# A gate table in memory: the last block's gates written by indirect transfers instead of one-hot products

## The reference, cut to what matters

```python
v1, i1 = lax.top_k(s1, 16); v2, i2 = lax.top_k(s2, 16)          # per token and head, over 128 keys each
cand = v1[:, None] + v2[None, :]; cidx = i1 * 128 + i2
top_s, pos = lax.top_k(cand, 16); eidx = cidx[pos]
gates = softmax(top_s)
act = gelu(u[eidx] . x)                                          # one number per token and chosen expert
y = sum over heads and choices of gates * act * v[eidx]
```

## Time and profile before

| | |
|---|---|
| median of 3 runs | 1862.31 us |
| the profiled execution | 1858.56 us |
| its span | 1856.8 us |
| PE busy | 1700.5 us (92%) |
| DVE busy | 1405.6 us (76%) |
| ACT busy | 694.7 us (37%) |
| POOL busy | 481.9 us (26%) |
| first and last rt_u_hi | 630.5 and 1277.1 us |

### The profile page before, as it was taken

The page is one execution under the profiler, slowest core; times in us unless marked ns, Lnnn a source line. Parts: engine busy times, 40 slices in busy tenths (PEclk is TensorE's granted clock), DMA queues, the critical chain, the costliest instruction groups (busy, mean ns, idle before and its releaser), DMA issues. The chain is left out here.

```text
span 1856.8 us, 28598 instructions
## 1 busy us (share of the span) xinstructions
PE 1700.5 (92%) x9877; PEld 1551.1 (84%) x9877; DVE 1405.6 (76%) x2543; ACT 694.7 (37%) x1050; POOL 481.9 (26%) x340
## 2 busy tenths in 40 slices
PE   6997778896879999999979998996999999999997
PEld 3875567554658899999979998996999999999996
DVE  4776766887342278999999998943888888888886
ACT  4664222325232234433334443432333333333333
POOL 1000000000110257877622332311332333322220
PEclk8999898888889999999989999998999999999999
DMA  3321000000213357887868887887999999999993
GB/s 107 101 81 55 1 1 35 23 1 1 91 57 101 129 156 241 291 274 264 269 222 322 324 322 257 321 291 270 330 369 393 371 377 380 374 369 335 355 348 107
DMA packets 149138, 404.56 MB, mean 218 GB/s; under 512 B 14100, under 2 KB 71700, under 8 KB 145592
## 3 DMA queue, kind: packets, MB, share of 16 engines
q1 hardware_dynamic: 108728, 243.99, 39.0%
q0 software_dynamic: 36864, 134.23, 19.1%
q10 hardware_dynamic: 3456, 25.17, 3.4%
HBM read 350.90 MB, written 52.44 MB: 217 GB/s over the span
## 5 line engine op out<-in xcount | busy, mean ns | idle before, releaser
L1579 PE MATMUL bank<-h_hi,rt_u_hi 128*128 128x384 f32 x1024 | 354.1, 346 | 24.7 <-DVE rt_u_lo L1364 13.4
L1744 PE MATMUL bank<-va_w_hi,va_v_hi 128*128 128x384 f32 x1024 | 342.9, 335 | 16.5 <-DVE va_w_lo L1695 16.5
L1581 PE MATMUL bank<-h_hi,rt_u_lo 128*128 128x384 f32 x1024 | 345.9, 338 | 0.1
L1580 PE MATMUL bank<-h_lo,rt_u_hi 128*128 128x384 f32 x1024 | 345.7, 338 | 0.0
L1745 PE MATMUL bank<-va_w_lo,va_v_hi 128*128 128x384 f32 x1024 | 342.7, 335 | 0.0
L1746 PE MATMUL bank<-va_w_hi,va_v_lo 128*128 128x384 f32 x1024 | 342.6, 335 | 0.0
L1294 ACT ACTIVATE rt_u_hi<-raw 128x1024 fp32r<-128x1024 f32 x128 | 135.7, 1061 | 385.9 <-PE bank L1581 385.6
L1672 ACT ACTIVATE va_v_hi<-raw 128x1024 fp32r<-128x1024 f32 x128 | 135.8, 1061 | 338.5 <-PE bank L1746 327.1
L1824 POOL DMA_INDIRECT h<-u_rows_dram,own_experts x128 | 172.0, 1344 | 279.5 <-DVE own_waste L1371 266.4
L1830 POOL DMA_INDIRECT qy<-v_dram,own_experts x128 | 129.8, 1014 | 373.1 <-DVE va_own L1722 368.4
L1579 PEld LDWEIGHTS bank<-h_hi,rt_u_hi 128*128 128x128 f32 x1024 | 195.2, 191 | 28.0 <-DVE rt_u_lo L1364 13.8
(11 more groups left out here) (328 smaller groups left out, 2733.5 us busy)
## 6 DMA issues: line engine op xcount, KB each, us to landing
raw<-u_dram SPq DMA_DIRECT2D x128, 512.0 KB, 4.1
raw<-v_dram SPq DMA_DIRECT2D x128, 512.0 KB, 7.0
active_scratch<-rt_act SPq DMA_DIRECT2D x128, 192.0 KB, 5.3
gates_scratch<-early ACTq DMA_DIRECT2D x24, 1024.0 KB, 7.4
early<-gates_scratch SPq DMA_DIRECT2D x16, 1536.0 KB, 12.4
early<-active_scratch SPq DMA_DIRECT2D x128, 192.0 KB, 7.6
in_raw<-w_in_dram SPq DMA_DIRECT2D x22, 512.0 KB, 3.4
query_raw<-w_query_dram SPq DMA_DIRECT2D x16, 512.0 KB, 3.5
```

The costliest lines, as they stand in the source:

```text
L1579: mm(bank, u_hi[:, j % 2, cols], hi[:, c, 0:TD], start=c == 0, stop=False)
L1580: mm(bank, u_hi[:, j % 2, cols], lo[:, c, 0:TD], start=False, stop=False)
L1581: last = mm(bank, u_lo[:, j % 2, cols], hi[:, c, 0:TD], start=False, stop=c == DC - 1)
L1744: mm(bank, v_hi[:, j, cols], w_hi[:, j, :], start=start, stop=False)
```

## The change

The table is built by one-hot products for two dense blocks only; the third dense block's gates go into the table by indirect transfers that add single elements in memory.

- Phase 1 has 32 steps (64 to 95, two bodies), phase 2 has 32 (96 to 127). All steps are written out; the hardware loop is gone from every engine but SP.
- Of the last block's slots no transpose, no `keep_slots` and no `split_gates` is made. `finish(3)` writes its gates to `single`, with tokens on partitions and slots along the row, and `list_experts(3)` computes for each slot its element number in the table, in two instructions (`place`).
- ACT issues, in step 19 (phase 0), one DMA that writes zeros over the last block's four chunks: 64 KB on each of 128 rows, 8.4 MB, from a zeroed buffer of 1 KB that is read 64 times.
- POOL issues 128 indirect DMAs, one per slot; each adds 128 elements of 4 bytes, one per token, to the table. They are put between the gathers: three behind each gather from gather 51 on. The first waits for the zeros, the places and the gates. Every 16th (one head's slots) waits until all before it have landed.
- SP waits for all 128 before it loads the gate table.
- The own dots: 48 in phase 0, 32 in phase 1 and 24 in phase 2 (12 per body).

```diff
+SPREAD = DENSE - 1
...
-    BODY, BODIES = 16, (4, DENSE, 1)
-    START = (0, 64, 112)
+    BODY, BODIES = 16, (NB, SPREAD, 2)
+    START = (0, 64, 96)
-    DOTS = (16, 16, 8)
-    FIRST_DOT = (0, 48, 96)
+    DOTS = (16, 16, 12)
+    FIRST_DOT = (0, 48, 80)
...
+        single, place = sb("single", [P, SLOTS]), sb("place", [P, SLOTS], U32)
+        empty = sb("empty", [P, 2 * P])
...
-            for j in range(BODY):
-                step(1, 0, j, True)
-            with eng.Fori(1, BODIES[1]) as i:
-                for j in range(BODY):
-                    step(1, i, j, False)
-            for j in range(BODY):
-                step(2, 0, j, True)
+            for phase in (1, 2):
+                for i in range(BODIES[phase]):
+                    for j in range(BODY):
+                        step(phase, i, j, i == 0)
...   (SP, after the last u loads)
-                    sp.wait_ge(sent[par], 16 * 2 * 2 * DENSE)
+                    sp.wait_ge(sent[par], 16 * 2 * 2 * SPREAD)
+                sp.wait_ge(s["scattered"], 16 * SLOTS)
...   (ACT)
-                    if phase == 1 and head and j == 4:
-                        keep_slots(NB - 1, t.bank[4])
+                    if phase == 0 and i == 1 and j == 3:
+                        act.wait_ge(s["empty"], 1)
+                        act.dma_start(gates_d[:, SPREAD * P // CH:TD // CH].rearrange("p c e n -> p (c e n)").rearrange(
+                            "p (k n) -> p k n", n=2 * P),
+                            empty[:].unsqueeze(1).to_broadcast([P, P * PK // (2 * P), 2 * P])).then_inc(s["cleared"], 16)
...   (POOL)
-                for k in range(START[1] - BODY, EARLY_DOTS + RING):
+
+                def scatter(k):
+                    if k == 0:
+                        pool.wait_ge(s["cleared"], 16)
+                        pool.wait_ge(s["places"], 1)
+                        pool.wait_ge(s["chosen"], NB)
+                    elif k % PTOP == 0:
+                        pool.wait_ge(s["scattered"], 16 * k)
+                    nc.gpsimd.indirect_dma_start(
+                        out=gates_d.rearrange("p c e (n one) -> (p c e n) one", one=1),
+                        out_offset=bass.IndirectOffsetOnAxis(ap=place[:, k:k + 1], axis=0),
+                        in_=single[:, k:k + 1], in_offset=None, compute_op=ALU.add).then_inc(s["scattered"], 16)
+
+                for at, k in enumerate(range(START[1] - BODY, EARLY_DOTS + RING)):
                     gather(k)
+                    for q in range(max(0, 3 * (at - 3)), min(SLOTS, 3 * (at - 2))):
+                        scatter(q)
...   (DVE)
+                    if i == NB - 1:
+                        place_f = num_f[:, 0].rearrange("p h k -> p (h k)")
+                        link(d.tensor_scalar(place_f, out[:, 0, :], float(TD * PK), t.vec[:, V_BASE:V_BASE + 1],
+                                             ALU.mult, ALU.add))
+                        d.scalar_tensor_tensor(place[:], out[:, 2, :], float(CH), place_f,
+                                               ALU.mult, ALU.add).then_inc(s["places"], 1)
...
-                    gates_out = out[:, 3, :] if i else gate_own[:]
+                    gates_out = (gate_own[:], out[:, 3, :], out[:, 3, :], single[:])[i]
...
+                d.memset(empty[:], 0.0).then_inc(s["empty"], 1)
...
-                    if phase == 1 and head and j == 6:
-                        split_gates(NB - 1)
...   (PE)
-                    if phase == 1 and head and j == 3:
-                        pe.wait_ge(s["moved"], 3)
-                        turn_slots(NB - 1, t.bank[4])
-                        pe.wait_ge(s["slots"], NB - 1)
```

More of the change, by code:

```diff
@@ L57 @@
 C_N = C_MT + LEVELS
-V_LN1, V_LN2, V_FIN, V_CONV, V_GDN, V_QN, V_KVN, V_IG, V_IB, V_EPS, V_ALOG, V_DTB, V_QK, V_ROWS, V_N = (
-    0, 8, 16, 24, 72, 73, 75, 77, 78, 79, 80, 84, 88, 96, 96 + 2 * 16)
+V_LN1, V_LN2, V_FIN, V_CONV, V_GDN, V_QN, V_KVN, V_IG, V_IB, V_EPS, V_ALOG, V_DTB, V_QK, V_ROWS, V_BASE, V_N = (
+    0, 8, 16, 24, 72, 73, 75, 77, 78, 79, 80, 84, 88, 96, 96 + 2 * 16, 97 + 2 * 16)
 CAND_ROWS = ((0, 1, 16), (1, 2, 8), (2, 4, 5), (4, 8, 3), (8, 16, 1))
@@ L1129, in route_stage @@
         "chain", "picked", "scores", "taken", "tops", "exps", "listed", "chosen", "turned", "slots_t", "slots",
-        "iota", "hots", "hot", "placed", "moved", "gelu", "kept")}
+        "iota", "hots", "hot", "placed", "moved", "gelu", "kept", "empty", "cleared", "places", "scattered")}
     with ExitStack() as ctx:
@@ L1155, in route_stage @@
         h_tok = t.pair
-        slot = sb("slot", [P, TD, 2, 2], BF16)
-        gate, rest = sb("gate", [P, TD]), sb("rest", [P, P])
-        piece = sb("piece", [P, 3, TD, 2], BF16)
+        slot = sb("slot", [P, SPREAD * P, 2, 2], BF16)
+        gate, rest = sb("gate", [P, SPREAD * P]), sb("rest", [P, P])
+        piece = sb("piece", [P, 3, SPREAD * P, 2], BF16)
+        single, place = sb("single", [P, SLOTS]), sb("place", [P, SLOTS], U32)
+        empty = sb("empty", [P, 2 * P])
         iota = sb("iota", [P, P], BF16)
@@ L1314, in step @@
                             send(i - 1, BODY + j - 2)
-                    if phase == 2:
+                    if phase == 2 and head:
                         if j < 2:
@@ L1929, in layout @@
     vec[:, V_ROWS:V_ROWS + 2 * PTOP] = row_tables()
+    last = SPREAD * P + np.arange(P)
+    vec[:, V_BASE] = last // CH * PK * CH + last % CH
     keys = np.stack([f["peer_sub_keys_1"][0], f["peer_sub_keys_2"][0]], axis=1)
```

## The result

The changed kernel takes 1931.13 us (median of 4 runs, 1926.39 to 1933.49), the kernel before 1861.87 us beside it: ratio 1.0365, 95% interval 1.0344 to 1.0386. 69 us slower where I had forecast 13 faster; the time lies 31 us above my range.

The account below looks back on a forecast made before the run. PE was taken to bound the kernel, with DVE close behind in phase 1. The terms -22.7 - 7.6 - 1.7 + 0.6 + 18 = -13.4 us gave 1845.2 profiled, 1849 us predicted as median; range 1829 to 1900.

Parts of the forecast that it names:

- Steps 1 to 5: Routing stage: sixteen steps' one-hot products -22.7 us, hardware loop -7.6, last block's transposes and slots -1.7, `place` +0.6, zero fill 0.
- Step 6, POOL's issue: Scatters on POOL between gathers: issues cost 0 in themselves, late start and waits for landings +18 us.
- POOL's issue: Rival, chance 0.12: 0.17 us more per issue makes groups miss low's end, 35 us more in phase 1, 1884 us.
- One gather and three scatters just fit a step: Phase 1 on POOL: four issues fit a 5.58 us step, with 0.67 us in hand that low takes back.
- The rule under it: On POOL, an indirect issue waits for DVE's tensor_tensor in progress, then takes 0.9 us beside the next.
- The waits every 16th: POOL's seven waits for landings, five in phase 1, taken at 4 us each: +18 us, with 2 us spare deducted.
- The start: Gather 52 goes 9.6 us late behind three scatters; of some 11.6 us to spare, 2 remain.
- Step 7: Scatters on the DMA engines, 1024 elements per engine: taken as 0, bounds 0 and +72 us.
- The fixed cost of a transfer: Estimate from the skill's page for the waits every 16th: 0.8 us each and 2 us lost.

Follow-up runs that it names:

- Plain writes: The changed kernel with scatters that write instead of add: 1888.03 us; with odd heads also sent to a second table (g 6.33 us): 1875.62 us.

## Why the prediction was wrong

**Steps 1 to 5 held.** Without scatters the change is worth 32.9 us, predicted 31.4; the loop 7.6 of it, as predicted; PE's wait at step 64 14.4 us, predicted 14.0. The zero fill landed after 74.5 us (predicted 71) with an issue of 0.44 us; I had taken 1.7 us for that issue. u loads beside it took 6.4 us in place of 3.9, and 7.6 at the longest, inside their time to spare. Neither the fill nor the sixteen steps were run alone, but nothing of the 32.9 us is missing, and in the run without scatters rt_u_hi starts every 4.16 us from step 98 on and every 5.58 in steps 68 to 71, as predicted.

**Step 6, POOL's issue, is the step that failed**, in three ways.

- *The price.* I gave a scatter the gather's 0.94 us because both have 128 indices. It takes 1.56. That the addition could cost was named in the rival, but only as the 0.17 us that would break the fit; it was 0.6. With it a group is over its time by its price alone: 0.94 + 3 x 1.56 and four gaps of 0.30 are 6.8 us, and 5.56 are there.
- *The fit.* "One gather and three scatters just fit a step" was a layout in which each issue arrived just before an instruction of DVE ended. Plain writes, with issues of 0.98 us, are the test: without waits for landings g is 6.33 us, and 6.41 between gathers 52 and 80, where POOL met no wait at all and the layout has 5.58. The rule under it was right. The scatter of 963.88 starts 0.1 us into a low, which ended at about 964.92, and is over at 966.44, 1.5 us later. That of 966.74 starts among the three gated instructions, 0.63 us each, close to the first one's end, and takes 1.55. The DVE rows for it:

```profile
963.78 1.22 DVE L1385 TENSOR_TENSOR rt_u_lo<-raw,rt_u_hi 128x1024 fp32r<-128x1024 f32 x1
964.92 1.22 DVE L1520 TENSOR_TENSOR qy<-rt_iota,rt_slot 128x2048 bf16<-128x2048 bf16 x1
966.17 1.90 DVE L1525 TENSOR_TENSOR qy<-qy,rt_piece 128x1024 bf16<-128x1024 bf16 x3
```

  But a wait of 0 to 1.1 us on each issue is a mean to be added, and not something that a layout makes vanish. In the changed kernel it is 0.12 us for a scatter and 0.38 for a gather, with plain writes 0.23 for a scatter.

  The Trainium skill ("SBUF — State Buffer", "Who interferes with whom") infers that a tensor_tensor doesn't stall descriptor generation; these rows are against it too.
- *The rival's price.* "POOL's issue" had the right mechanism and a chance of 0.12, but I priced it by a single missed boundary, 1.25 us a step, 1884. The rows I had would have bounded it: four issues of 1.81 us and four gaps of 0.30 make 8.4 us, against 5.56 an extra 2.9 us for each of 43 groups, and a high end beyond 1931. A range that ended at 1900 left that out. I also priced it for phase 1 alone, since phase 2 had 5.55 us for a group of 4.96; there a group took 7.4 (gathers 80 to 94).

**The waits every 16th** were sized well: 25.0 us in 6 places are 4.2 us each, I took 4 (the seventh met none), and taking them away gave 27 us. They didn't decide the outcome: POOL was over its time without them, and that run was still 2.1% slower than the kernel before. In *The start* 21.1 - 9.2 is 11.9 and not 11.6; it changes nothing.

**Step 7 held** for the scatters that add. The DMA share fell, from 0.88 to 0.79, gathers landed sooner than before, and clearings that send nothing lie on the same line as the scatters.

**The fixed cost of a transfer**, about 2 us in the Trainium skill ("DMA: Bandwidth & Descriptors", "Anatomy of one DMA — SWDGE (gpsimd) path"), would by my estimate have made the waits 0.8 us each; the six here were 0.7 to 6.3.

## What to carry to other kernels

Work moved to an engine that "has room" must be measured against the queue it joins: add up all that the queue must issue between two items that others wait for, at the dearest price that the trace shows for such an instruction, and compare it with the period of the consumer. Below the period it is free (1832 us), above it every tenth of a microsecond comes back times the number of groups (42 here), and the idle time that it makes can also cost the clock (31 of the 104 us). And where a change bundles several edits, run the cheap one alone: writing the loop out gave 1855 us, which the whole change doesn't reach.

## What the runs showed of the hardware

- An indirect DMA that adds holds POOL for 1.56 us, one that writes for 0.98, at 128 elements of 4 bytes; at 64 elements the adding one still takes 1.44.
- An indirect issue that starts while DVE runs a tensor_tensor on two buffers ends 0.9 us (gather) or 1.5 us (adding scatter) after that instruction's end. One that starts under the dot isn't held: 15 adding scatters of the changed kernel did, and took 1.55 to 1.56 us.
- A POOL tensor_tensor of 128x512 slows DVE's bf16 tensor_tensor of 128x1024 from 0.69 to 1.66 us in the mean (960 to 1110 us); clearing 128x1024 on POOL doesn't (0.69).
- One DMA of 8192 pieces of 1 KB was issued in 0.44 us and landed in 74.5 us.
- Behind 6.87 us without a product PE's granted clock was 0.50 for 3.4 us (the lower level, 1.2 GHz), and products of 128x384 started every 0.32 us instead of every 0.17.
- The backward jump of a hardware loop with 16 steps in its body cost 7.6 us; written out, the steps cost nothing.
